# Seven block products in place of eight for 18 of 22 weight pairs of the second feed-forward input

## Chip, core and metric

The kernel runs on one NeuronCore of a Trainium2 chip (TensorE = PE, VectorE = DVE, ScalarE = ACT, GpSimd = POOL, SyncE = SP). The metric is the device time in microseconds (us) of one execution, lower is better; the median of several runs counts.

## The reference

One layer of a hybrid backbone on 128 context tokens and 512 noisy tokens, 640 columns in all, each of width 1024. The layer is a first SwiGLU feed-forward block, a mixer (short convolution and gated DeltaNet), and a second SwiGLU block, each with a modulated RMS norm ahead and a gated residual behind. The change lies in the second block:

```python
def _swiglu(h, w_in, w_out):
    a, b = jnp.split(h @ w_in, 2, axis=-1)
    return (jax.nn.silu(a) * b) @ w_out
...
    h = _rmsnorm(x, norm_ffn2) * (1 + sc3) + sh3
    x = x + 0.5 * gt3 * _swiglu(h, w_ffn2_in, w_ffn2_out)
```

`w_ffn2_in` is 1024 by 5632 (a and b of 2816 columns each), `w_ffn2_out` is 2816 by 1024. All is float32.

## The kernel before

Activations lie transposed: features on the 128 partitions, the 640 tokens as columns, so a feature vector of 1024 is KD = 8 tiles and the inner width 2816 is KF = 22 tiles. Float32 accuracy comes from splitting each operand in a high part (`_hi`, rounded to PE's fast float32r form) and a low part (`_lo`, the rest), and adding three products: hi*hi, hi*lo and lo*hi.

A **unit** is one column tile of weights (128 columns, all 8 k tiles): `load_w` (SP, L335) brings 512 KB into a slot of `w_raw`, `split_hi` (ACT, L942) and `split_lo` (DVE, L1266) make `w_hi` and `w_lo`, and `unit` (PE, L521) issues 8 k tiles * 3 products * 2 halves of the tokens = 48 matmuls:

```python
for n, (w, m) in enumerate(((wh, hi), (wh, lo), (wl, hi))):
    for b in range(2):
        last = pe.matmul(to[a_slot][b], w, m[:, k0 + k, part[b]],
```

The two halves (320 columns and 322) go to two PSUM banks in turn. The columns past the 640th hold the norm's shift, so the norm's scale 1/rms can be applied after the product. There are two weight slots and two accumulators.

A **pair** is unit a and unit b of the same 128 inner features. For a pair, DVE multiplies both results with `rinv` out of PSUM (`scaled`, L1336, two instructions for each unit), ACT takes silu with the shift as bias (`gate_in`, L1018), and DVE forms (b + shift) * silu (`shifted`, L1354), then g_hi (L1376) and g_lo (L1378). The second block's input stage is 22 such pairs, in a hardware loop from pair 2 on. Each engine's order is that of the code; semaphores (`mm_done`, `hi_ready`, `lo_ready`, `acc_free`) hold the engines together.

The stage opens with `sum_squares(2)` (L536) after its first unit and `spread(2)` (L543) after its second, by which 1/rms gets onto all partitions; ACT copies it out (L995, L996). The **output stage** (`swiglu_out`) follows: for each of 8 output tiles j three weight units of 8, 7 and 7 k tiles, 132 matmuls, then five transposes of the tile before (`turn_y`, L923). For j = 0 each k tile waits until its g_hi and g_lo are there (`g_rdy`).

Of the kernel before, what the change touches and what calls it, by code (L numbers as in the profile page):

```python
# [45 lines left out]
KO = ((0, 8), (8, 15), (15, 22))  # L46
HEADS = 4
# [23 lines left out]
U_F2O = U_F2I + 2 * KF  # L71
# [7 lines left out]
A_F2O = A_F2I + 2 * KF  # L79
# [31 lines left out]
def hybrid_layer(nc, x_prompt, x_sample, state_f, state_b, c, c_ctx, w_ada, b_ada, norm1, w1i, w1o, norm_mix,  # L111
# [3 lines left out]
    with ctx:  # L115
# [107 lines left out]
        def view(t, dims):  # L223
# [15 lines left out]

        ps = [ctx.enter_context(nc.psum_tensor(f"ps{i}", [P, 512], F32)) for i in range(8)]  # L240
# [18 lines left out]
        misc_set, vec_tr, vec_rdy, c_rdy = sem("misc_set"), sem("vec_tr"), sem("vec_rdy"), sem("c_rdy")  # L259
# [67 lines left out]
        def _(sp):  # L327
# [87 lines left out]
            for n in range(28):  # L415
                col = strip_col(n)
                load_w(U_MI + n, n % 2, w_mi_v[:, :, col:col + P], KD)
                if n == 1:
# [9 lines left out]
                                 ).then_inc(in_adt, 16)  # L428
                    sp.dma_start(gsm["adt"][:, 8:16], dt_bias.rearrange("a b h -> a (b h)").to_broadcast([P, 8])
                                 ).then_inc(in_adt, 16)  # L430
# [65 lines left out]
            with sp.Fori(0, KF) as i:  # L496
                for b in range(2):
                    load_w(U_F2I + 2 * i + b, b, w_in_v[1][:, :, bass.ds(P * i + b * FF, P)], KD)
            load_out(U_F2O, w_out_v[1])
# [4 lines left out]
            sp.wait_ge(out_done, 16 * NC)  # L504
            sp.wait_ge(st_done, 32)
# [3 lines left out]
        def _(pe):  # L509
            def unit(u, slot, kt, hi, lo, a_slot, start=True, stop=True, k0=0, h_wait=None, wide=True, ks=None):  # L510
# [3 lines left out]
                for k in ks or range(kt):  # L514
# [4 lines left out]
                    for n, (w, m) in enumerate(((wh, hi), (wh, lo), (wl, hi))):  # L519
                        for b in range(2):  # L520
                            last = pe.matmul(to[a_slot][b], w, m[:, k0 + k, part[b]],  # L521
                                             start=start and k == 0 and n == 0,
                                             stop=stop and k == kt - 1 and n == 2)
                last.then_inc(mm_done, 1)
# [51 lines left out]
            pe.wait_ge(c_rdy, 1)  # L576
# [60 lines left out]
            def swiglu_out(u0, a0, g0, after=lambda j: None):  # L637
                for j in range(KD):
                    s = j % 2
                    acc_wait(a0 // 2 + j // 2, s)  # L640
# [5 lines left out]
            swiglu_out(U_F1O, A_F1O, 0)  # L646
# [37 lines left out]
            for n in range(2, 28):  # L684
# [21 lines left out]
                if n == 12:  # L706
# [5 lines left out]
                    last.then_inc(ab_tr, 1)  # L712
                if n == 14:

                    pe.wait_ge(dve_g, 1)
                    pe.wait_ge(in_tri, 48)
# [192 lines left out]
            unit(U_F2I + 1, 1, KD, h_hi, h_lo, 1)  # L909
            spread(2)  # L910
# [3 lines left out]
            with pe.Fori(2, KF) as i:  # L914
                swiglu_in(i, U_F2I, A_F2I)

# [10 lines left out]
            swiglu_out(U_F2O, A_F2O, KF, after=lambda j: turn_y(j - 1) if j > 0 else None)  # L927
# [4 lines left out]
            last.then_inc(y_sum, 1)  # L932
# [3 lines left out]
        def _(act):  # L936
# [11 lines left out]
            for row, v in ((R_N1, norm1[0]), (R_NM, norm_mix[0]), (R_N2, norm2[0]), (R_NF, norm_f)):  # L948
# [14 lines left out]
                                 ).then_inc(c_rdy, 1)  # L963
# [79 lines left out]
            def swiglu_out(u0, n0, more, x0, after):  # L1043
                for j in range(KD):
                    split_out(u0, 3 * j + 1)
# [29 lines left out]
            for n in range(28):  # L1075
# [4 lines left out]
                if n == 13:  # L1080

                    act.wait_ge(ab_rdy, 3)
                    nc.scalar.activation(gsm["t1"][:, :, :, :], gsm["t1"][:, :, :, :], ACT.Exp).then_inc(act_g, 1)
                    nc.scalar.activation(gsm["beta"][:, :, :, :], gsm["t3"][:, :, :, :], ACT.Exp).then_inc(act_g, 1)
                    act.wait_ge(in_adt, 32)
# [4 lines left out]
                if n == 15:  # L1090
                    act.wait_ge(dve_g, 2)
                    nc.scalar.activation(gsm["gl"][:, :, :, :], gsm["gt"][:, :, :, :], ACT.Exp)
                    nc.scalar.activation(gsm["kgs"][:, :, :, :], gsm["t2"][:, :, :, :], ACT.Exp).then_inc(gates, 1)  # L1093
# [70 lines left out]
            for n in range(-1, NC):  # L1164
# [7 lines left out]
                if n == 0:  # L1172
# [4 lines left out]
                    for d, out in enumerate((s_out_f, s_out_b)):  # L1177
                        act.wait_ge(s_rdy[d], 1)
                        act.dma_start(out[0, 0].rearrange("h k v -> k h v"), Sb[d][:, :, :]).then_inc(st_done, 16)
# [27 lines left out]
            act.wait_ge(st_done, 32)  # L1207
# [53 lines left out]
        def _(dve):  # L1261
# [192 lines left out]
            def gates_first():  # L1454

                dve.wait_ge(ab_tr, 1)
                dve.wait_ge(in_adt, 32)
                ab4 = G["ab"][:, :].rearrange("p (c a h) -> p a c h", c=NC, a=4)
                link(nc.vector.tensor_copy(G["ab"][:, :], ps[6][:, 0:NC * NAB]))
                for d in range(2):  # L1460
# [5 lines left out]
                                        ).then_inc(ab_rdy, 1)  # L1466
# [436 lines left out]
```

## Time and profile before

| | |
|---|---|
| three runs, us | 1514.38, 1517.43, 1517.10 (median 1517.1) |
| the profiled execution, us | 1514.96 |
| its span in the trace, us | 1513.1 |
| PE busy | 1445.8 us, 96% of the span |
| DVE busy | 690.1 us, 46% |
| ACT busy | 401.7 us, 27% |
| SP's hardware DMA queue | 153.06 MB, 32.7% of 16 engines |
| mean granted PE clock | 0.979 |

An engine's busy time is the time in which it had an instruction under way; matmuls overlap, so PE's rate is read from the distance between starts or from the length of a run of matmuls. The clock is given as a share of 2.4 GHz. A number in square brackets behind a row of the timeline is the time that the engine stood idle before it, with what ended it.

### The profile page before, as it was taken

How to read it: one execution, taken by the hardware profiler on the slowest of the kernel's cores; microseconds unless marked ns; L12 is line 12 of the kernel's file. 1: busy time of each engine (PE TensorE's matmuls, PEld its weight loads, DVE VectorE, ACT ScalarE, POOL GpSimd, SP SyncE). 2: the span in 40 equal slices, each digit the busy share in tenths (PEclk: the TensorE clock that was granted, in tenths of full speed). 3: DMA queues.
4: the chain of work that ended last, by engine and by line, in shares of the span. 5: the costliest groups of instructions: out<-in, count | busy, mean ns of one | idle time of the engine just before them, and what ended most of it. 6: DMA issues, size and time to landing. Idle time of an engine off the chain costs nothing.

```text
span 1513.1 us, 24131 instructions
## 1 busy us (share of the span) xinstructions
PE 1445.8 (96%) x9932; PEld 1398.4 (92%) x9932; DVE 690.1 (46%) x1203; ACT 401.7 (27%) x596; POOL 112.9 (7%) x92
## 2 busy tenths in 40 slices
PE   5899999999999999999987999899999999999996
PEld 2787899999999999999986999899999999999996
DVE  2433344444323326566476665554444354442222
ACT  3321112122122226553222212232221221222222
POOL 0000000000000000002342664000000000000000
PEclk9899999999999999999998999999999999999998
DMA  9687522222222222222544333021222222222222
GB/s 342 247 297 274 166 67 80 68 73 74 72 77 77 74 72 70 70 57 84 158 135 124 104 91 88 15 84 57 83 69 69 83 69 69 83 63 77 77 67 80
DMA packets 221459, 154.73 MB, mean 102 GB/s; under 512 B 22437, under 2 KB 208206, under 8 KB 217294
## 3 DMA queue, kind: packets, MB, share of 16 engines
q1 hardware_dynamic: 219936, 153.06, 32.7%
q8 instruction: 52, 0.85, 0.2%
q10 hardware_dynamic: 1454, 0.68, 0.2%
q14 instruction: 17, 0.14, 0.0%
HBM read 140.47 MB, written 13.24 MB: 102 GB/s over the span
## 4 chain that ended last, share of the span: by engine, by line
PE 90%; DVE 4%; DMA 1%; ACT 1%; POOL 1%; issue 1%; SPq 1%; ACTq 0%; DVEq 0%; POOLq 0%
PE ps L521 72%; PE ps L883 3%; PE ps L563 2%; PE ps L755 2%; PE ps L767 1%; PE ps L766 1%; PE ps L594 1%; DMA w_raw<-in_w_ffn_in 1%; DVE sub_tmp L1534 1%; PE ps L869 1%; PE ps L802 1%; DVE sub_x L1537 1%; POOL Tm L1834 1%; DVE ss L1610 1%; PE ps L804 1%
## 5 line engine op out<-in xcount | busy, mean ns | idle before, releaser
L521 PE MATMUL ps<-h_hi,w_hi 128*128 128x320 f32 (+1 forms) x1824 | 427.1, 315 | 3.1 <-DVE w_lo L1266 3.1
L521 PE MATMUL ps<-h_lo,w_hi 128*128 128x320 f32 (+1 forms) x1824 | 421.7, 312 | 0.0
L521 PE MATMUL ps<-h_hi,w_lo 128*128 128x320 f32 (+1 forms) x1824 | 420.4, 312 | 0.0
L942 ACT ACTIVATE w_hi<-w_raw 128x1024 fp32r<-128x1024 f32 (+1 forms) x172 | 178.7, 1040 | 808.4 <-PE ps L521 742.9
L521 PEld LDWEIGHTS ps<-h_hi,w_hi 128*128 128x128 f32 x1824 | 310.0, 190 | 17.0 <-issue 12.9
L521 PEld LDWEIGHTS ps<-h_hi,w_lo 128*128 128x128 f32 x1824 | 309.9, 190 | 0.0
L521 PEld LDWEIGHTS ps<-h_lo,w_hi 128*128 128x128 f32 x1824 | 309.2, 190 | 0.0
L1266 DVE TENSOR_TENSOR w_lo<-w_raw,w_hi 128x1024 fp32r<-128x1024 f32 (+1 forms) x172 | 207.9, 1209 | 185.3 <-ACT w_hi L942 181.5
L1336 DVE TENSOR_TENSOR pn<-ps,rinv 128x320 f32<-128x320 f32 (+1 forms) x144 | 64.1, 487 | 274.3 <-PE ps L521 263.5
L521 PE MATMUL ps<-g_hi,w_hi 128*128 128x320 f32 x704 | 160.7, 310 | 0.0
L521 PE MATMUL ps<-g_hi,w_lo 128*128 128x320 f32 x704 | 160.5, 309 | 0.0
L521 PE MATMUL ps<-g_lo,w_hi 128*128 128x320 f32 x704 | 160.5, 309 | 0.0
L521 PEld LDWEIGHTS ps<-g_hi,w_lo 128*128 128x128 f32 x704 | 117.8, 188 | 0.0
L521 PEld LDWEIGHTS ps<-g_hi,w_hi 128*128 128x128 f32 x704 | 117.6, 188 | 0.0
L521 PEld LDWEIGHTS ps<-g_lo,w_hi 128*128 128x128 f32 x704 | 117.5, 188 | 0.0
L1336 DVE TENSOR_TENSOR sa<-ps,rinv 128x320 f32<-128x320 f32 x88 | 39.2, 487 | 133.5 <-PE ps L521 115.1
L1406 DVE SCALAR_TENSOR_TENSOR x<-ps,gate,x 128x128 f32<-128x128 f32 (+2 forms) x72 | 27.2, 434 | 89.8 <-PE ps L521 66.9
L1816 POOL TENSOR_TENSOR DT<-tri,s_g 128x512 f32<-128x512 f32 x10 | 11.3, 1138 | 754.6 <-ACT s_kgs L1093 686.7
L1354 DVE SCALAR_TENSOR_TENSOR pn<-pn,sa 128x128 f32<-128x128 f32 x88 | 44.7, 549 | 4.3 <-ACT sa L1018 1.1
L1171 ACT ACTIVATE Xm<-ps 128x512 f32<-128x512 f32 x30 | 17.9, 597 | 99.3 <-PE ps L755 99.3
L1018 ACT ACTIVATE sa<-sa 128x128 f32<-128x128 f32 x88 | 44.1, 548 | 0.0
L767 PE MATMUL ps<-Rm,Xm 128*128 128x128 f32 x240 | 41.5, 279 | 0.0
(233 smaller groups left out, 1289.2 us busy)
## 6 DMA issues: line engine op xcount, KB each, us to landing
w_raw<-in_w_ffn_in SPq DMA_DIRECT2D x88, 512.0 KB, 3.7
ada_w<-in_w_ada SPq DMA_DIRECT2D x32, 1024.0 KB, 6.5
w_raw<-in_w_ffn_out SPq DMA_DIRECT2D x32, 448.0 KB, 3.5
w_raw<-in_w_mix_in SPq DMA_DIRECT2D x28, 512.0 KB, 3.7
w_raw<-in_w_ffn_out SPq DMA_DIRECT2D x16, 512.0 KB, 3.8
ada_w<-in_w_ada SPq DMA_DIRECT2D x8, 512.0 KB, 4.0
w_raw<-in_w_mix_out SPq DMA_DIRECT2D x8, 512.0 KB, 5.1
d_lt<-LTp SPq DMA_DIRECT2D x10, 256.0 KB, 2.2
```

The source lines that it names most:

```text
L521: last = pe.matmul(to[a_slot][b], w, m[:, k0 + k, part[b]], start=start and k == 0 and n == 0, stop=stop and k == kt - 1 and n == 2)
L563: last = pe.matmul(adap[32 * g:32 * g + 32, 0:width], ccol[:, k, :], ada_w[:, s, g * width:(g + 1) * width], start=k == 0, stop=k == KD - 1)
L755: last = pe.matmul(hs(bank[d][3], h), nt[:, h, :], Tm[d][:, h, :], start=True, stop=True)
L767: last = pe.matmul(hs(bank[d][2], h), Xm[d][:, h, :], R[:, h, :], start=True, stop=True)
L883: last = pe.matmul(acc[s][b], w, m[:, k % 4, PART[b]], start=k == 0 and n == 0, stop=k == KD - 1 and n == 2)
L942: nc.scalar.activation(w_hi[:, slot, 0:kt * P], w_raw[:, slot, 0:kt * P], ACT.Copy).then_inc(hi_ready, 1)
L1018: last = nc.scalar.activation(sa[:, t0:t1], sa[:, t0:t1], ACT.Silu, bias=sa[:, T + g:T + g + 1])
L1171: nc.scalar.activation(flat(Xm[d]), bank[d][3][:, :], ACT.Copy).then_inc(xm_rdy[d], 1)
L1266: nc.vector.tensor_tensor(w_lo[:, slot, 0:kt * P], w_raw[:, slot, 0:kt * P], w_hi[:, slot, 0:kt * P].bitcast(F32), ALU.subtract).then_inc( ...
L1336: last = nc.vector.tensor_tensor(dst[:, PARTW[b]], accw[a_slot][b], rinv[:, PARTW[b]], ALU.mult)
L1354: last = nc.vector.scalar_tensor_tensor(out=dst[:, t0:t1], in0=pn[:, t0:t1], scalar=pn[:, T + g:T + g + 1], in1=other[:, t0:t1], op0=ALU.a ...
L1406: last = nc.vector.scalar_tensor_tensor(out=x[:, j, t0:t0 + b1 - b0], in0=acc[a_slot][bnk][:, b0:b1], scalar=gate[:, m, j, i:i + 1], in1=x ...
```

## The change

The first NP0 = 4 pairs stay as they are. The other NSP = 18 pairs are each computed as a 2 by 2 block product: the weights in halves of k (0 to 3, 4 to 7) and in a and b, the activations in the same halves of k and in the two token halves (320 each). Seven products of 4 k tiles and 320 columns take the place of eight (Strassen's scheme in Winograd's form): 7 * 4 * 3 = 84 matmuls for a pair in place of 96. They need four sums of weight blocks for each pair (`S1` to `S4f`, DVE), four sums of activation blocks made once (`T1` to `T4`, DVE), and sums of products: five on DVE out of PSUM (u2, u3, c22, c21, c12), and three in PSUM, where products 4, 5 and 6 accumulate on the banks of products 0, 2 and 3. ACT copies product 0 out first (p1), and takes silu of c11 and c12.

For that the normed, scaled and shifted h must exist in float32 (`hf`): during the first four pairs DVE multiplies x by 1/rms (8 of 640 columns) and ACT applies gain and shift (16 instructions). Each of the seven activation operands is split in hi and lo once (1280 columns), each of the seven weight operands for every pair (512 columns each).

The weights of even pairs load into `w_raw`, those of odd pairs into `w_more` (a part of the old `h` buffers), as two DMAs of 512 KB each. Eight PSUM banks serve two pairs in turn, four each. The product g stays float32 (`g32`) through the stage, one DVE multiplication of 640 columns for a pair; hi and lo of all 22 tiles are made at the end (`halve_hi` on ACT, `halve_lo` on DVE, 22 each), partly over the memory of the block operands. Some semaphores of other stages are merged, with the waits at the same places. `spread(2)` moves into the middle of the second unit.

```diff
-            with pe.Fori(2, KF) as i:
+            for i in range(2, NP0):
                 swiglu_in(i, U_F2I, A_F2I)
+            def product(s, p, to, w, v, again=False):
+                pe.wait_ge(op_rdy, 7 * s + (p + 1))
+                for k in range(4):
+                    wh, wl = (t[:, k * P:k * P + P] for t in w[0:2])
+                    for n, (a, m) in enumerate(((wh, v[0]), (wh, v[1]), (wl, v[0]))):
+                        last = pe.matmul(to, a, m[:, k, :], start=not again and k == 0 and n == 0, stop=k == 3 and n == 2,
+                                         skip_group_check=again)
+                last.then_inc(pr_done, 1)
...
+                product(s, 0, X, A11, b11_g if first else B11)
...
+                product(s, 1, Y, S2, T2)
...
+                product(s, 2, Z, S3, T3)
...
+                product(s, 3, W, S1, T1)
+                pe.wait_ge(*p1_rdy(s))
...
+                product(s, 4, X, A12, B21, again=True)
+                pe.wait_ge(*u3_rdy(s))
+                product(s, 5, Z, A22, T4, again=True)
+                pe.wait_ge(*c22_rdy(s))
...
+                product(s, 6, W, S4, B22, again=True)
```

SP and DVE (the first load of a block pair waits for the last `split_lo` of the old form):

```diff
+            sp.wait_ge(lo_ready, U_F2O)
+            load_pair(0, 0, first(0))
...
+            sums_of(0, 0, None)
+            part_lo(3, T4, T4[2][:, :, :])
+            last_sum(0, 0)
+            unit_scaled(6, 0)
+            part_lo(4, b11_g, block(0, 0))
+            operand_lo(0, 0, A11, w_raw[:, 0, 0:HW4])
...
+            for k in range(0, 6):
+                halve_lo(k)
+            dve.wait_ge(pr_done, 7 * NSP)
+            nc.vector.tensor_tensor(c12, u2, xyzw[1][3], ALU.add).then_inc(dve_ev, 1)
+            split_out(U_F2O, 0)
...
+            split_out(U_F2O, 1)
+            for k in range(12, KF):
+                halve_lo(k)
```

What DVE does for a pair inside its loop. Before, one pass of the loop (`sa`, `pn` results of a and b, `w_lo` the two weight units, `g` the product):

```order
L1266 TENSOR_TENSOR w_lo<-w_raw,w_hi 128x1024 [waits hi_ready]
L1361 REGISTER_ALU
L1336 TENSOR_TENSOR sa<-ps,rinv 128x320 [waits mm_done]
L1336 TENSOR_TENSOR sa<-ps,rinv 128x322
L1265 REGISTER_ALU
L1266 TENSOR_TENSOR w_lo<-w_raw,w_hi 128x1024 [waits hi_ready]
L1336 TENSOR_TENSOR pn<-ps,rinv 128x320 [waits mm_done]
L1336 TENSOR_TENSOR pn<-ps,rinv 128x322
```

In the change, the first part of one pair (`sa` here is c12 of the pair before; `rinv` is u2, `S_` and `A_` are weight operands, `g_171` is g32):

```order
L2111 TENSOR_TENSOR sa<-rinv,ps 128x320 [waits pr_done]
L2091 REGISTER_ALU
L2092 TENSOR_TENSOR S_lo<-S_sum,S_hi 128x512 [waits oh_rdy]
L2091 REGISTER_ALU
L2092 TENSOR_TENSOR A_lo<-w_raw,A_hi 128x512 [waits oh_rdy]
L2096 REGISTER_ALU
L2097 REGISTER_ALU [waits act_ev]
L2098 REGISTER_ALU [waits act_ev]
L2103 ISA [waits dve_ev]
L2103 TENSOR_TENSOR g_171<-sa,pn 128x640
L2117 ISA [waits pr_done]
L2121 REGISTER_ALU [waits act_ev]
```

Longer instructions have become shorter ones with more register steps and waits between them; a whole pair has 17 DVE instructions that compute.

DVE at the seam to the output stage. Before, the last rows of the loop and the first behind it:

```order
L1378 REGISTER_ALU [waits gh_rdy]
L1378 TENSOR_TENSOR g_lo<-pn,g_hi 128x640
L1778 REGISTER_ALU
L1778 COMPARE_AND_BRANCH
L1266 TENSOR_TENSOR w_lo<-w_raw,w_hi 128x896 [waits hi_ready] x2
```

In the change, from the last pair's c21 on:

```order
L2143 TENSOR_TENSOR pn<-rinv,ps 128x320 [waits pr_done]
L2166 TENSOR_TENSOR g_lo<-g_171,g_hi 128x640 [waits gh_rdy] x6
L2172 TENSOR_TENSOR sa<-rinv,ps 128x320 [waits pr_done]
L1503 TENSOR_TENSOR w_lo<-w_raw,w_hi 128x1024 [waits hi_ready]
L2166 TENSOR_TENSOR g_lo<-g_171,g_hi 128x640 [waits gh_rdy] x3
L2103 TENSOR_TENSOR g_171<-sa,pn 128x640 [waits dve_ev,act_ev]
L2166 TENSOR_TENSOR g_lo<-g_171,g_hi 128x640 [waits gh_rdy] x3
L1503 TENSOR_TENSOR w_lo<-w_raw,w_hi 128x896 [waits hi_ready]
L2166 TENSOR_TENSOR g_lo<-g_171,g_hi 128x640 [waits gh_rdy] x10
L1503 TENSOR_TENSOR w_lo<-w_raw,w_hi 128x896 [waits hi_ready]
```

The low part of the output stage's first weight unit (the first `w_lo` row) now stands behind six g_lo and the sum c12, and 16 more g_lo follow it.

## Rows read from the trace of the kernel before

**Rows 1.** The page, chain that ended last: shares of the span by engine and line.
```profile
PE 90%; DVE 4%; DMA 1%; ACT 1%; POOL 1%; issue 1%; SPq 1%; ACTq 0%; DVEq 0%; POOLq 0%
PE ps L521 72%; PE ps L883 3%; PE ps L563 2%; PE ps L755 2%; PE ps L767 1%; PE ps L766 1%; PE ps L594 1%; DMA w_raw<-in_w_ffn_in 1%; DVE sub_tmp L1534 1%; PE ps L869 1%; PE ps L802 1%; DVE sub_x L1537 1%; POOL Tm L1834 1%; DVE ss L1610 1%; PE ps L804 1%
```

**Rows 2.** Windows: stretch, us, then busy of each engine, granted clock, DMA share, GB/s.
```profile
1075.00:1210.00 135.00, 135.00 (x910) 135.00 (x909) 60.35 (x93) 29.16 (x39) 0.00 (x0) 1.00 0.26 76
```

**Rows 3.** Timeline of DVE, one pair of the loop: start, length, instruction, idle before.
```profile
1303.42 0.89 DVE L1336 TENSOR_TENSOR sa<-ps,rinv 128x320 f32<-128x320 f32 x2 [2.39 <-PE ps L521]
1304.51 1.22 DVE L1266 TENSOR_TENSOR w_lo<-w_raw,w_hi 128x1024 fp32r<-128x1024 f32 x1 [0.20 <-ACT w_hi L942]
1310.56 0.89 DVE L1336 TENSOR_TENSOR pn<-ps,rinv 128x320 f32<-128x320 f32 x2 [4.82 <-PE ps L521]
1311.57 1.02 DVE L1354 SCALAR_TENSOR_TENSOR pn<-pn,sa 128x128 f32<-128x128 f32 x2
1312.73 0.49 DVE L1376 CAST g_hi<-pn 128x640 f32 x1
1313.34 0.82 DVE L1378 TENSOR_TENSOR g_lo<-pn,g_hi 128x640 f32 x1
1314.09 1.22 DVE L1266 TENSOR_TENSOR w_lo<-w_raw,w_hi 128x1024 fp32r<-128x1024 f32 x1
1317.70 0.49 DVE L1336 TENSOR_TENSOR sa<-ps,rinv 128x320 f32<-128x320 f32 x1 [2.39 <-PE ps L521]
```

**Rows 4.** The chain in order of time, output stage: start, us, what.
```profile
1377.79 0.55 PE ps L923 x5
1378.34 19.36 PE ps L521 x132
1397.70 0.55 PE ps L923 x5
```

**Rows 5.** Groups by form, 640 us to the end: count, busy us, mean ns, idle before.
```profile
L1266 DVE TENSOR_TENSOR w_lo<-w_raw,w_hi 128x1024 fp32r<-128x1024 f32 x76 | 94.6, 1246 | 45.9 <-ACT w_hi L942 44.8
L1336 DVE TENSOR_TENSOR pn<-ps,rinv 128x320 f32<-128x320 f32 x40 | 19.6, 491 | 141.0 <-PE ps L521 139.3 <-issue 1.6
L1378 DVE TENSOR_TENSOR g_lo<-pn,g_hi 128x640 f32 x20 | 16.5, 825 | 2.5
L1703 DVE TENSOR_TENSOR Rm<-Rm,ps 128x512 f32<-128x512 f32 x30 | 20.3, 682 | 6.4 <-PE ps L767 6.3
L1171 ACT ACTIVATE Xm<-ps 128x512 f32<-128x512 f32 x30 | 17.9, 597 | 99.3 <-PE ps L755 99.3
```

**Rows 6.** The page, DMA issues: count, KB each, us to landing.
```profile
w_raw<-in_w_ffn_in SPq DMA_DIRECT2D x88, 512.0 KB, 3.7
ada_w<-in_w_ada SPq DMA_DIRECT2D x32, 1024.0 KB, 6.5
```

**Rows 7.** Timeline at the opening of the second block's input stage.
```profile
1037.76 1.23 PEld L543 LDWEIGHTS ps<-ident,rms 128*128 128x128 f32 x10
1039.22 0.60 ACT L995 ACTIVATE rinv<-ps 128x512 f32<-128x512 f32 x1 [7.14 <-PE ps L543]
1039.71 0.27 ACT L996 ACTIVATE rinv<-ps 128x128 f32<-128x128 f32 x1
```

**Rows 8.** Timeline of PE: two waits elsewhere in the kernel.
```profile
569.57 0.78 PE L521 MATMUL ps<-h_hi,w_hi 128*128 128x320 f32 x2 [3.06 <-DVE w_lo L1266]
826.38 2.05 PE L755 MATMUL ps<-Tm,NTa 128*128 128x128 f32 x8 [5.58 <-POOL NTa L1843]
```

**Rows 9.** Windows behind those two waits, columns as in rows 2.
```profile
570.00:575.00 5.00, 5.00 (x26) 5.00 (x25) 3.02 (x7) 4.07 (x6) 0.00 (x0) 0.69 0.37 105
826.00:832.00 6.00, 5.43 (x24) 5.17 (x25) 0.00 (x0) 1.19 (x2) 6.00 (x6) 0.50 0.27 55
832.00:836.00 4.00, 4.00 (x34) 3.92 (x33) 2.04 (x4) 0.00 (x0) 4.00 (x5) 0.93 0.06 15
```

**Rows 10.** Timeline of PE, products in plain float32 (two instructions each, same columns).
```profile
889.92 2.01 PE L767 MATMUL ps<-Rm,Xm 128*128 128x128 f32 x16
```

More of the change, by code:

```diff
@@ L908, in _ @@
             acc_wait(A_F2I // 2, 1)
-            unit(U_F2I + 1, 1, KD, h_hi, h_lo, 1)
-            spread(2)
+            unit(U_F2I + 1, 1, KD, h_hi, h_lo, 1, between=lambda k: spread(2) if k == 3 else None)
             unit(U_F2I + 2, 0, KD, h_hi, h_lo, 2)
@@ new lines, in hi_last, with seven @@
+            def hi_last(s, q, free):
+                act.wait_ge(*free[0])
+                operand_hi(s, 5, A22, (w_raw, w_more)[q][:, 1, HW4:])
+                act.wait_ge(*free[1])
+                act.wait_ge(sum_rdy, 4 * s + 4)
+                operand_hi(s, 6, S4, S4f[:, :])
+            def seven(s, q, prep=True):
+                X, Y, Z, W = xyzw[q]
+                first = isinstance(s, int) and s == 0
+                if not first:
+                    act.wait_ge(*c12_rdy(s - 1))
+                    nc.scalar.activation(c12, c12, ACT.Silu).then_inc(act_ev, 1)
+                act.wait_ge(pr_done, 7 * s + 1)
+                if not first:
+                    act.wait_ge(*u2_rdy(s - 1))
+                nc.scalar.activation(p1, X, ACT.Copy).then_inc(act_ev, 1)
+                hi_last(s, q, ((mm_done, U_F2O),) * 2 if first else ((pr_done, 7 * s - 1), (pr_done, 7 * s)))
+                if first:
+                    part_hi(5, B21, hf[:, 4:KD, 0:TH])
+                    part_hi(6, B22, hf[:, 4:KD, TH:T])
+                    for i in range(2):
+                        act.wait_ge(vlo, 5)
+                        nc.scalar.activation(B11[i][:, :, :], b11_g[i][:, :, :].bitcast(F32), ACT.Copy).then_inc(vhi, 1)
+                if prep:
+                    hi_a11(s + 1, 1 - q, (pr_done, 7 * s + 1))
+                act.wait_ge(pr_done, 7 * s + 5)
+                act.wait_ge(*g_made(s + (NP0 - 1)))
+                nc.scalar.activation(c11, X, ACT.Silu).then_inc(act_ev, 1)
+                if prep:
+                    hi_four(s + 1, 1 - q, (pr_done, 7 * s + 5))
@@ new lines, in _, with halve_hi @@
+            hi_a11(0, 0, (mm_done, U_F2O - 1))
+            gate_in(3, A_F2I, KF)
+            hi_four(0, 0, (mm_done, U_F2O - 1))
+            seven(0, 0)
+            with act.Fori(0, NSP // 2 - 1) as r:
+                for q in (1, 0):
+                    seven(2 * r + (2 - q), q)
+            seven(NSP - 1, 1, prep=False)
+            def halve_hi(k):
+                last = 7 * (NSP - 1)
+                act.wait_ge(pr_done, last + (2 if k < 4 else 3 if k < 8 else 4 if k < 12 else 6))
+                if k >= 20:
+                    act.wait_ge(op_rdy, 7 * NSP)
+                act.wait_ge(*g_made(k))
+                nc.scalar.activation(g2_hi[:, k, :], g32[:, k, :], ACT.Copy).then_inc(gh_rdy, 1)
```

400 lines of the change are left out of this document (336 added, 64 removed).

## The prediction

> **What bounds the kernel now.** I read the chain that ended last first [rows 1]: 90% of it is PE, 72% the matmuls of L521, so what counts is how many matmuls there are, how far apart they start, and where PE waits. The window in the middle of the stage that changes [rows 2] shows PE busy for all of its 135 us at the full clock of 2.4 GHz, DVE for 60 us and ACT for 29. The timeline of DVE [rows 3] gives the period of a pair, from one result `sa` to the next: 1317.70 - 1303.42 = 14.28 us for 96 matmuls, 148.75 ns each (320 and 322 columns in turn). In the output stage, where all have 320 columns, 132 take 19.36 us [rows 4]: 146.67 ns each. The profiled execution took 1514.96 us, its span 1513.1; the median of the three runs, 1517.1, is 2.1 above it.
>
> **What the change takes from PE.** A block pair has 84 matmuls of 320 columns: 84 * 0.14667 = 12.32 us for 14.28, that is 1.96 us less; for 18 pairs **-35.3 us**, if PE stays without waits. That prices the same 128-row weight load and the same float32r columns as in rows 4. What differs is that the 12 matmuls of a product follow each other in one bank, where now two banks alternate. The trace has no float32r row of that. In the nearest rows [rows 10] a plain float32 product is two instructions into the same columns of a bank, 16 in 2.01 us, 115 ns each and no gap. So I take 0, between a gain of 0 and the loss of the second rival. TensorE's own rate is also the place to weigh a rule: the Trainium skill, page "TensorE: Matmul & The Clock Gate", section "Back-to-back issue gap", gives columns / 2.4 GHz + 2.5 ns, 135.8 ns for 320 columns. Rows 4 show 146.67. By the page the pair would save 13.08 - 11.41 = 1.67 us and the stage 30.1; I stay with the rows.
>
> **Does DVE keep up inside the loop?** A block pair has 17 computing DVE instructions. Five sums out of PSUM at 0.49 us, one product of 640 columns at 0.825 [rows 5]; eleven of 512 columns out of SBUF (four sums, seven low parts), priced at 0.70, between the 0.682 of a 512-column operation with a PSUM operand and the line through 640 and 1024 columns (0.825 and 1.246) [rows 5]. Sum 2.45 + 0.825 + 7.7 = 10.97 us, against 12.32 of PE. Back to back it is less: independent neighbours overlap by about 0.07 (w_lo starts at 1314.09, g_lo would end at 1314.16) [rows 3], so 9.8. ACT has seven copies of 512 at 0.60 and three of 320 at about 0.5: 5.7 us. I laid the three engines' orders side by side with these durations, 0.1 us from one of them to the next and 0.2 from PE or to PE. Counted from a pair's product 0: c12 at 0.2, S1 and A12 low parts by 1.9, the g product by 2.7, u2 at 3.7 (product 1 ends at 3.5), u3 at 5.5, c22 at 7.2, S1, S3, S2, the next pair's A11 and S4f by 10.8, c21, S2 and S3 low parts by 12.5. The next product 0 needs A11's low part, ready at 10.2, at 12.3; product 1 needs S2's at 14.1, ready at 11.9. Everything is about 2 us early, each pair alike, so in the loop **0**. Weights: a pair's load starts 4.9 us into the pair but one before it, and is wanted at 20.0, 15 us later; two DMAs of 512 KB in series would take 2 * 3.7 = 7.4 [rows 6]. Hidden, with half the time to spare.
>
> **The opening.** `spread(2)` moves, its cost (1.2 us of PE) stays. But DVE now does `scaled` for unit 0 and two of the x * 1/rms before it makes w_lo of unit 2. Spread ends 3.57 us of matmuls before unit 1 does; ACT copies 1/rms out in about 0.8 [rows 7]; then 0.89 + 2 * 0.755 + 1.16 on DVE (each less its overlap) and 0.2 to PE, 4.9 us against 3.57: **+1.3**.
>
> **The seam into the block pairs.** The first block load is issued only when the last w_lo of the old form is made, about 9.4 us before unit 7, the last old one, ends. For its two DMAs of 512 KB I take the 6.5 us of the row of 1024 KB, between 3.7 (all in parallel) and 7.4 (in series) [rows 6]. Behind it DVE has S1, S3, S2 (2.0), T4's low part (1280 columns, 1.42), S4f (0.63), `scaled` (0.82), B11's low part (1.42), A11's (0.63), in all 6.9, and 0.3 for the hand-overs: 6.5 + 6.9 + 0.3 - 9.4 = **+4.3** in front of product 0 (1.5 to 5.2). Product 4 then waits for B21's low part: **+0.55**.
>
> **The seam to the output stage.** Let E be the end of the last product. DVE's c21 starts at E - 1.56 (product 5 is done), ends at about E - 1.15; six g_lo at 0.755 take it to E + 3.4, c12 to E + 3.8, w_lo (1.16) to E + 5.0. PE starts at **+5.2**; before, it started at once. Then PE takes 0.88 us for a k tile, DVE 0.755 for a g_lo, but it has the last g product and w_lo of the second unit in between, and w_lo of the third comes behind g_lo 21, at E + 19.9, where PE wants it at E + 18.4 (k tile 15): **+1.7**. The 22 g_lo and casts that leave the loop are in these terms; in the loop they were hidden. The cover for all of this is the matmuls of j = 0; it is too short by 1.7.
>
> **The clock.** Waits of that size have a second price. After 3.06 us of waiting [rows 8] the granted clock was 0.69 in the next 5 us, with 26 matmuls [rows 9], where 5 / 0.14875 = 33.6 fit: 1.1 us lost. After 5.58 us [rows 8] it was 0.50 for 6 us and 0.93 for the next four [rows 9], 1.2 GHz for some 6.3 us; 320 columns at 1.2 GHz are 267 ns, for 147, so 6.3 * (1 - 147/267) = 2.8 lost. I take 1.1 for the wait of 4.3 and 2.8 for that of 5.2. A slow PE lets DVE catch up, so the small waits behind them (0.55, 1.7) vanish: net 3.9 - 2.25 = **+1.7**.
>
> **The sum:** -35.3 + 1.3 + 4.3 + 0.55 + 5.2 + 1.7 + 1.7 = -20.5, so 1514.96 - 20.5 = 1494.4. Because the profiled execution lies 2.1 below the median, I add half of that: **1495.5 us**. Merged semaphores and earlier stages cost nothing; their waits stand where they stood. That the change does less than it says is excluded: 216 fewer matmuls are issued.
>
> **Rivals.** A measurement of this kernel can tell about 0.2%, 3 us, from no change.
>
> *DVE becomes the bound in the loop, and the kernel slower.* For: in the loop DVE's dependent instructions start 0.12 to 0.15 us after their forerunner's end (1311.57, 1312.73, 1313.34) [rows 3], with one register step and one wait between; the new loop has up to four. If every one of the 17 pays such a gap of 0.2 and overlaps nothing, a pair is 10.97 + 3.4 = 14.4 us, the gain 35.3 - 18 * 2.05 = -1.6, and with the seams' 14.8 the kernel takes 1532. The kernel gets slower from a period of 14.28 - 14.8/18 = 13.5, a gap of 0.15. Against: the one independent follower in the loop, w_lo with its wait already fulfilled, shows no gap but an overlap, and in the new order each dependent pair has another instruction between. The Trainium skill, page "VectorE: DVE Perf Modes", section "The TRN2 errata", states a fixed extra cost for each instruction, so that many small ones pay more; by it this rival is likelier than the one row makes it. 9%.
>
> *One bank for 12 matmuls costs PE time.* 1512 matmuls; 25 ns each would be +38, 1533 us, and 14 ns already take the whole gain. Against it stand rows 10 without a gap. 3%.
>
> *Partly bound.* A gap of 0.1 without overlap makes DVE's period 12.7, +6; with somewhat slower cross-engine steps, seams of 18 to 20 us in all and a longer slow clock this ends between 1502 and 1513, say 1506. 17%.
>
> *Shorter seams.* The first load lands in 3.7 us, no clock falls at the first wait, DVE overlaps more: 1485 to 1489. 7%.
>
> **How the numbers follow.** Forecast 62% (1489 to 1502 by the load's ends and the clock's), shorter seams 7%, partly bound 17%, back to within 0.2% of before 2%, slower 12% (9 and 3). So faster 0.86, same 0.02, slower 0.12. The range leaves out the slower cases and some of the partly bound at the top, and the very best at the bottom: 1486 to 1511.
>
> **What would show it.** Pairs 12.3 us apart in the new loop and PE without idle time there; DVE busy for about 9.8 us of each. Three waits of PE: about 1.3 before unit 2, 4 before the first block product (released by a low part of DVE after a weight load), 5 before the output stage (released by w_lo). Granted clock below 1 behind the last two. The output stage from j = 1 on as in rows 4. Wrong would be: a period over 12.6 us; waits on `op_rdy` in every pair; 84 matmuls that take over 12.4 us without idle time (the bank); or seams of more than 20 us.

## The result, and the profile after

| | before | changed |
|---|---|---|
| median, us | 1517.26 (4 runs, 1514.38 to 1518.69) | 1492.64 (4 runs, 1489.5 to 1493.57) |
| ratio to before | | 0.9835, 95% interval 0.9819 to 0.9851 |
| the profiled execution, us | 1514.96 | 1493.57 |
| its span, us | 1513.1 | 1491.8 |
| PE busy, us | 1445.8 | 1416.8 |
| DVE, ACT busy, us | 690.1, 401.7 | 779.5, 472.0 |
| mean granted PE clock | 0.979 | 0.975 |

The change makes the kernel 1.65% faster. The forecast was 1495.5, in a range of 1486 to 1511.

The chain that ended last, changed kernel, from the stage's first unit to the output stage (start, us, what; it answers to [rows 4]):

```profile
1024.00 7.14 PE ps L583 x48
1032.15 3.68 PE ps L583 x24
1075.26 5.02 DMA w_raw<-in_w_ffn_in
1087.15 8.73 PE ps L986 x48
1096.14 212.99 PE ps L986 x1452
1309.65 4.41 DVE g_lo L2166 x6
1315.84 40.40 PE ps L583 x264
1356.79 19.36 PE ps L583 x132
```

L986 is the block product, L583 every other feed-forward matmul. The row of 1452 carries the gain: 212.99 / 1452 = 146.69 ns a matmul, without a break over 17 pairs. The chain leaves PE for long only twice, for the first block load and for the six g_lo with the w_lo behind them. The shares in the profile page's chain say the same: PE fell from 90% [rows 1] to 88%, DVE rose from 4% to 5%.

PE's waits in the stage, from its timeline (the bracket is the idle time before, with its releaser; the kernel before had no waits at these places):

```profile
1041.33 0.56 PE L583 MATMUL ps<-h_hi,w_hi 128*128 128x320 f32 x2 [0.80 <-DVE w_lo L1503]
1087.15 0.60 PE L986 MATMUL ps<-b_hi,A_hi 128*128 128x320 f32 x1 [2.71 <-DVE A_lo L2092]
1096.14 0.39 PE L986 MATMUL ps<-B_hi,A_hi 128*128 128x320 f32 x1 [0.27 <-issue]
1315.84 0.87 PE L583 MATMUL ps<-g_hi,w_hi 128*128 128x320 f32 x2 [4.96 <-DVE w_lo L1503]
```

Windows of the changed kernel, columns as in [rows 2]: the two places behind the long waits, and the middle of the loop.

```profile
1087.00:1090.00 3.00, 2.85 (x11) 2.88 (x12) 2.96 (x7) 1.13 (x3) 0.00 (x0) 0.50 0.86 239
1130.00:1290.00 160.00, 160.00 (x1094) 160.00 (x1093) 126.16 (x221) 66.37 (x131) 0.00 (x0) 1.00 0.30 85
1315.80:1319.80 4.00, 3.96 (x17) 3.99 (x18) 4.00 (x6) 4.00 (x7) 0.00 (x0) 0.59 0.39 115
```

In the loop PE is busy for all of the 160 us at the full clock, as in [rows 2], with DVE at 79% where it had 45%. Behind both waits the granted clock is 0.50 to 0.59 in these windows, that is 1.2 GHz for most of them, and matmuls run 267 ns apart (in product 0 from 1087.55 to 1087.82 and on): product 0 takes 1090.44 - 1087.15 = 3.29 us, the first 12 of the output stage as much (1315.84 to 1319.13). Each time that is 1.53 us more than 12 * 0.14667 = 1.76. This is what one execution shows; the experiments below show that the price of the clock isn't the same in each.

DVE in the loop, one pair from c12 (`sa`) on, which answers to [rows 3]:

```profile
1163.24 0.49 DVE L2111 TENSOR_TENSOR sa<-rinv,ps 128x320 f32<-128x320 f32 x1
1163.64 0.68 DVE L2092 TENSOR_TENSOR S_lo<-S_sum,S_hi 128x512 fp32r<-128x512 f32 x1
1164.24 0.68 DVE L2092 TENSOR_TENSOR A_lo<-w_raw,A_hi 128x512 fp32r<-128x512 f32 x1
1164.85 0.82 DVE L2103 TENSOR_TENSOR g<-sa,pn 128x640 f32 x1
1167.06 0.49 DVE L2122 TENSOR_TENSOR rinv<-ssq,ps 128x320 f32<-128x320 f32 x1 [1.39 <-PE ps L986]
1167.46 0.68 DVE L2092 TENSOR_TENSOR A_lo<-w_raw,A_hi 128x512 fp32r<-128x512 f32 x1
1168.70 0.49 DVE L2128 TENSOR_TENSOR rinv<-rinv,ps 128x320 f32<-128x320 f32 x1 [0.55 <-PE ps L986]
1169.10 0.68 DVE L2092 TENSOR_TENSOR S_lo<-S4f,S_hi 128x512 fp32r<-128x512 f32 x1
1170.45 0.49 DVE L2135 TENSOR_TENSOR pn<-rinv,ps 128x320 f32<-128x320 f32 x1 [0.66 <-PE ps L986]
```

DVE stands idle 1.39 + 0.55 + 0.66 = 2.6 us a pair, always for a product, never for ACT or a load. An instruction of 512 columns lasts 0.68, but the next starts 0.60 behind it (1163.64, 1164.24). The register steps and the fulfilled waits between them (each pair of rows here has them) take no time that the timeline shows. Such gaps were what the slower rival rested on. The Trainium skill, page "VectorE: DVE Perf Modes", section "The DRAIN you can't avoid", says that a semaphore after each DVE instruction costs nothing extra; the trace agrees, with 0.60 a step across such waits.

**Where the time went**, against the kernel before. Its stage starts at 1022.68 (chain) and its unit 2 at 1038.94 (timeline of PE):

```profile
1022.68 7.14 PE ps L521 x48
1038.94 0.54 PE L521 MATMUL ps<-h_hi,w_hi 128*128 128x320 f32 x2
```

(The profiled execution of the changed one enters the stage 1.3 us later, 1024.00 against 1022.68; the versions below, which differ in nothing ahead of it, enter it anywhere from 1021.51 to 1025.30.)

| step | us | worked out |
|---|---|---|
| 1512 matmuls for 1728 | -35.3 | 18 * (14.28 - 12.32) |
| unit 2's wait | +1.07 | starts 17.33 after the stage's first unit, before 16.26 |
| wait before product 0 | +2.98 | unit 7 would have ended at 1041.33 + 6 * 7.14 = 1084.17, product 0 starts at 1087.15 |
| slow clock there | +1.53 | 3.29 for 1.76 |
| B21's low part | +0.27 | the row at 1096.14, see e_dve_a |
| wait before the output stage | +5.0 | the row at 1315.84 |
| slow clock there | +1.53 | 3.29 for 1.76 |
| sum | -22.9 | |

From the stage's first unit to the first `turn_y` (the five transposes, L923 before, L1036 now) the chains give 1377.79 - 1022.68 = 355.11 and 1356.25 - 1024.00 = 332.25: -22.86. So the sum leaves nothing of this execution unexplained. I call this stretch the **stage length**. It is read from one profiled execution of each kernel. It doesn't hold what whole executions differ by ahead of the stage and behind it, so it is the sharper measure below: the same kernel gives 332.25 and 332.00 (again), or 324.44 and 324.47 (v_all, v_all_b). It does hold the clock, which can move it by a microsecond or more.

### The profile page after: what moved, and what is told of

The parts are those of the page before. It is cut to its first block, busy times and chain, and to the rows that moved or that the text cites. A ratio compares the mean times of both kernels' runs of the same rounds, so it can differ in the third digit from the quotient of the medians.

```text
span 1491.8 us, 24430 instructions
## 1 busy us (share of the span) xinstructions
PE 1416.8 (95%) x9716; PEld 1368.1 (92%) x9716; DVE 779.5 (52%) x1362; ACT 472.0 (32%) x751; POOL 112.9 (8%) x92
## 4 chain that ended last, share of the span: by engine, by line
PE 88%; DVE 5%; DMA 2%; POOL 1%; ACT 1%; issue 1%; SPq 1%; ACTq 0%; DVEq 0%; POOLq 0%
PE ps L583 55%; PE ps L986 15%; PE ps L947 3%; PE ps L626 2%; PE ps L819 2%; PE ps L831 1%; PE ps L830 1%; DMA w_raw<-in_w_ffn_in 1%; PE ps L657 1%; DVE sub_tmp L1772 1%; PE ps L933 1%; PE ps L866 1%; POOL Tm L2236 1%; DVE sub_x L1775 1%; DVE w_lo L1503 1%
## 5 line engine op out<-in xcount | busy, mean ns | idle before, releaser
L583 PE MATMUL ps<-h_hi,w_hi 128*128 128x320 f32 x1248 | 295.1, 318 | 3.9 <-DVE w_lo L1503 3.9
L583 PE MATMUL ps<-h_lo,w_hi 128*128 128x320 f32 x1248 | 288.6, 313 | 0.0
L583 PE MATMUL ps<-h_hi,w_lo 128*128 128x320 f32 x1248 | 288.3, 312 | 0.0
L583 PEld LDWEIGHTS ps<-h_hi,w_hi 128*128 128x128 f32 x1248 | 212.5, 190 | 18.0 <-issue 12.9
L583 PEld LDWEIGHTS ps<-h_hi,w_lo 128*128 128x128 f32 x1248 | 212.5, 190 | 0.0
L583 PEld LDWEIGHTS ps<-h_lo,w_hi 128*128 128x128 f32 x1248 | 211.9, 190 | 0.0
L583 PE MATMUL ps<-g_hi,w_hi 128*128 128x320 f32 x704 | 161.6, 311 | 5.0 <-DVE w_lo L1503 5.0
L583 PE MATMUL ps<-g_hi,w_lo 128*128 128x320 f32 x704 | 160.9, 310 | 0.0
L583 PE MATMUL ps<-g_lo,w_hi 128*128 128x320 f32 x704 | 160.8, 310 | 0.0
L1573 DVE TENSOR_TENSOR pn<-ps,rinv 128x320 f32<-128x320 f32 x108 | 48.1, 487 | 173.7 <-PE ps L583 162.8
L583 PEld LDWEIGHTS ps<-g_hi,w_hi 128*128 128x128 f32 x704 | 118.1, 189 | 5.2 <-issue 5.2
L583 PEld LDWEIGHTS ps<-g_lo,w_hi 128*128 128x128 f32 x704 | 118.3, 189 | 0.0
L583 PEld LDWEIGHTS ps<-g_hi,w_lo 128*128 128x128 f32 x704 | 118.1, 189 | 0.0
L986 PE MATMUL ps<-T_hi,S_hi 128*128 128x320 f32 x216 | 66.7, 309 | 0.0
L986 PE MATMUL ps<-T_hi,S_lo 128*128 128x320 f32 x216 | 66.7, 309 | 0.0
L986 PE MATMUL ps<-T_lo,S_hi 128*128 128x320 f32 x216 | 66.7, 309 | 0.0
```

What stands on the lines that cost most here:

```text
L583: last = pe.matmul(to[a_slot][b], w, m[:, k0 + k, part[b]], start=start and k == 0 and n == 0, stop=stop and k == kt - 1 and n == 2)
L986: last = pe.matmul(to, a, m[:, k, :], start=not again and k == 0 and n == 0, stop=k == 3 and n == 2, skip_group_check=again)
L1573: last = nc.vector.tensor_tensor(dst[:, PARTW[b]], accw[a_slot][b], rinv[:, PARTW[b]], ALU.mult)
```

## Experiments

All were run on chips with the kernel before beside them. Ratios are to that kernel, with the 95% interval. There were three groups: again, e_inseam, e_outseam and v_all (before: 1515.94); e_dve_a, e_dve_b, e_eight and e_open (1517.05); v_all2 and v_all_b (1516.96).

| run | median, us | ratio | stage length, us |
|---|---|---|---|
| again | 1493.7 | 0.9843 (0.983 to 0.9857) | 332.00 |
| e_dve_a | 1493.39 | 0.9846 (0.9822 to 0.9871) | 333.02 |
| e_dve_b | 1510.34 | 0.9958 (0.994 to 0.9976) | 348.71 |
| e_eight | 1523.15 | 1.0046 (1.003 to 1.0061) | 360.78 |
| e_open | 1493.07 | 0.9844 (0.9821 to 0.9867) | 331.97 |
| e_inseam | 1489.23 | 0.9825 (0.9812 to 0.9838) | 327.74 |
| e_outseam | 1489.29 | 0.9822 (0.9803 to 0.9841) | 328.94 |
| v_all | 1485.72 | 0.9799 (0.9786 to 0.9813) | 324.44 |
| v_all_b | 1487.1 | 0.9799 (0.9776 to 0.9823) | 324.47 |
| v_all2 | 1482.06 | 0.9773 (0.9752 to 0.9793) | 320.98 |

**again**, the changed kernel unedited, as the base of the others.

> The changed kernel once more, as the yardstick of this chip. Both theories: ratio to before about 0.984 to 0.986 (24.6 us less by the medians so far, 21.4 by the profiled executions); in the trace again three waits of PE in the second input stage, about 0.8, 2.7 and 5.0 us, and a loop period of 12.3 us.

It repeats: 1493.7, with the same waits (0.80, 2.5, 5.0).

### Is the loop bound by PE, and by how much?

**e_dve_a and e_dve_b**: a reduction on DVE in every pair, 1500 or 3600 columns, whose result nobody reads.

```diff
                 if not first:
                     gate_pair(s - 1)
+                nc.vector.tensor_reduce(ssq[:, TH:TH + 1], x[:, :, :].rearrange("p k t -> p (k t)")[:, 0:3600],
+                                        mybir.AxisListType.X, ALU.add)
                 dve.wait_ge(pr_done, 7 * s + 2)
```

> One more DVE instruction in each of the 18 block pairs, behind the g product: a sum over 1500 columns of x into a spare column, about 1.6 us, whose result nobody uses. Forecast's theory (DVE has 2.6 us to spare in a period of 12.3 and the operands are 2 us early): no more than 2 us slower in all, period 12.3. Rival (DVE near its bound): period 13 or more, 12 us slower or more.

> The same with 3600 columns, about 3.8 us. Forecast's theory: DVE's 9.8 us become 13.6, so DVE is the bound, period 13.6 us, PE waits in every pair, about 23 us slower than the changed kernel, which is the time of the kernel before (1513 to 1520). A theory in which waits between the engines add to the sums gives 14 us and more for a pair, over 30 us slower.

The small one costs nothing that can be measured, though DVE's busy time in the middle of the loop rises from 126.16 to 146.04 of 160 us. The window of e_dve_a:

```profile
1130.00:1290.00 160.00, 160.00 (x1094) 160.00 (x1093) 146.04 (x235) 66.32 (x130) 0.00 (x0) 1.00 0.30 85
```

The stage length is 1.0 longer than in again, but not by waits of PE for the loaded DVE: the clock makes the difference. The chain of e_dve_a has these two rows, where the changed kernel has 8.73 and 40.40:

```profile
1086.06 7.28 PE ps L986 x48
1314.50 41.55 PE ps L583 x264
```

The waits before them are nearly those of the change (2.58 for 2.71, and 4.96), but the granted clock isn't: behind the first it stayed at 1.00, and behind the second it was 0.50 until 5.7 us after the restart, where in the change it was back at 1.00 after 3.2. The first saves 1.45 us, the second costs 1.15. (e_eight below has 7.28 at the first place too, behind a wait of 2.68.)

What the load on DVE does cost is in the first pair, ahead of product 4. There PE waits 1.48 us where the change had 0.27, both times put down to "issue". DVE's timeline names the releaser: B21's low part ends at 1093.23 + 1.48 = 1094.71 in e_dve_a, and product 4 starts at 1094.82; from the timelines of DVE and of PE in e_dve_a,

```profile
1093.23 1.48 DVE L2040 TENSOR_TENSOR B_lo<-hf,B_hi 128x1280 fp32r<-128x1280 f32 x1
```

```profile
1094.82 0.39 PE L986 MATMUL ps<-B_hi,A_hi 128*128 128x320 f32 x1 [1.48 <-issue]
```

In the changed kernel that low part runs from 1094.56 to 1096.04, and product 4 starts 0.10 behind its end, at 1096.14. In e_dve_b it ends at 1098.46 and the product starts at 1098.57. So the 0.27 is the prediction's wait for B21, and "issue" here is a wait whose releaser the profile didn't find.

Set against the changed kernel's own profile (333.02 for 332.25, 0.8 longer), e_dve_a has 1.21 more for this wait, 0.13 less for the wait before product 0, 1.45 less and 1.15 more for the clock. From product 4 on the loop costs nothing more: 1452 matmuls take 212.98 us in e_dve_a and 212.99 in the change.

With the large one DVE is busy for all of the window, PE is not, and PE waits once in every pair. First the same window of e_dve_b, then its rows of PE's waits in the stage (engine line <- releaser: us in total, times, longest us):

```profile
1130.00:1290.00 160.00, 153.06 (x1025) 149.94 (x1024) 160.00 (x221) 61.23 (x123) 0.00 (x0) 1.00 0.28 80
```

```profile
PE ps L986 <- DVE rinv L2130: 9.6, 17, 0.7
PE ps L583 <- ACT sa L1480: 5.0, 1, 5.0
```

The wait before the output stage stays at 5.0, under another releaser. The period is 13.16 us in place of 12.32. From the timeline of DVE in e_dve_b:

```profile
1147.31 3.89 DVE L2116 TENSOR_REDUCE ssq<-x 128x1 f32<-128x3600 f32 x1
1151.13 0.47 DVE L2124 TENSOR_TENSOR rinv<-ssq,ps 128x320 f32<-128x320 f32 x1
...
1160.47 3.89 DVE L2116 TENSOR_REDUCE ssq<-x 128x1 f32<-128x3600 f32 x1
```

The reduction takes 1151.13 - 1147.31 = 3.82 of the period, so the pair's own 17 instructions, packed with nothing idle, take 13.16 - 3.82 = 9.34 us. The prediction had 9.8, and the same excess is why this run came out below the 1513 to 1520 that it was expected to take. In the loop of the change DVE could thus do 12.32 - 9.34 = 3.0 us more for each pair (worked out; e_dve_a takes about 1.6 of it at no cost, and the 3.82 of e_dve_b are too much).

**e_eight**: 12 more matmuls a pair, ahead of product 6. One of the four results of a pair is therefore another one.

```diff
+                for k in range(4):
+                    wh, wl = (t[:, k * P:k * P + P] for t in A22[0:2])
+                    for a, m in ((wh, T4[0]), (wh, T4[1]), (wl, T4[0])):
+                        pe.matmul(W, a, m[:, k, :], start=False, stop=False, skip_group_check=True)
                 product(s, 6, W, S4, B22, again=True)
```

> Twelve more matmuls in each block pair, as an eighth product would have: A22 and T4 once more, into the bank of product 6, so that one of the four results is another one. Forecast's theory (PE's matmuls are all that the loop costs, one bank or not): 18 * 1.76 = 31.7 us slower than the changed kernel, period 14.08, no waits in the loop. If the loop had hidden slack of its own on another engine, less: 25 or below.

The chain of e_eight in the loop is PE alone:

```profile
1280.55 12.31 PE ps L986 x84
1292.85 1.76 PE ps L1024 x12
```

An eighth product costs 1.76 us a pair in full; the kernel is then slower than before, by 0.46%. Of the 18 * 1.76 = 31.7 us the medians show 29.5 (1523.15 - 1493.7) and the stage length 28.8. The wait before the output stage is 3.2 here, not 5.0, since DVE gets 1.76 us more before the end, and in the profiled execution the clock didn't fall in the first seam (7.28 for 8.73). Together with e_dve_b this gives the point at which the kernel turns slower, too: ratios 0.9958 at a period of 13.16 and 1.0046 at 14.07 cross 1 at 13.16 + 0.91 * 42 / 88 = 13.6. The prediction put it at 13.5.

### The two seams

**e_inseam**: the low parts that need no weights come ahead of the weight sums.

```diff
-            sums_of(0, 0, None)
             part_lo(3, T4, T4[2][:, :, :])
-            last_sum(0, 0)
             unit_scaled(6, 0)
             part_lo(4, b11_g, block(0, 0))
+            sums_of(0, 0, None)
+            last_sum(0, 0)
```

> DVE makes the low parts of T4 and B11 and unit 6's result ahead of the first weight sums, while the first block load is in flight. Theory A (DVE's order behind the load makes the 2.7 us): the wait before the first block product goes to 0, and with it the slow clock of its 12 matmuls, together 4 to 4.5 us less than the changed kernel. Theory B (the load's landing sets the seam): sums start at the same time, but the wait stays over 1.5 us and less than 2 us is won.

The wait is gone, and no slow matmuls follow. The chain of e_inseam:

```profile
1039.01 43.11 PE ps L583 x288
1082.12 7.04 PE ps L986 x48
1089.15 0.27 issue
1089.42 212.99 PE ps L986 x1452
```

48 block matmuls take 7.04 us where the change took 8.73. The stage length falls by 332.0 - 327.74 = 4.3, against 2.98 + 1.53 = 4.5 in the table. The 0.27 of B21 stays. So the wait hung on DVE's order, as theory A had it. In the change DVE stands idle 4.10 us for the load and only then makes 1.48 + 1.48 us of low parts that don't need it:

```profile
1074.72 1.48 DVE L2040 TENSOR_TENSOR T_lo<-T_sum,T_hi 128x1280 fp32r<-128x1280 f32 x1
1080.30 0.69 DVE L2078 TENSOR_TENSOR S_sum<-w_raw 128x512 f32<-128x512 f32 x1 [4.10 <-DMA w_raw<-in_w_ffn_in]
...
1082.12 1.48 DVE L2040 TENSOR_TENSOR T_lo<-T_sum,T_hi 128x1280 fp32r<-128x1280 f32 x1
...
1084.92 1.48 DVE L2040 TENSOR_TENSOR b_lo<-hf,b_hi 128x1280 fp32r<-128x1280 f32 x1
```

**e_outseam**: in the last pair, ACT makes the high parts of six g tiles and of the first output unit ahead of c11; DVE makes three g_lo, that unit's low part and another g_lo ahead of c21. DVE's part of the edit:

```diff
+                else:
+                    for k in range(0, 3):
+                        halve_lo(k)
+                    split_out(U_F2O, 0)
+                    halve_lo(3)
                 dve.wait_ge(pr_done, 7 * s + 6)
...
-            for k in range(0, 6):
+            for k in range(4, 6):
                 halve_lo(k)
...
-            split_out(U_F2O, 0)
```

> The last pair makes the first six g_hi and the high part of the first output weight unit ahead of its c11 (ACT), and DVE makes four g_lo and that unit's low part ahead of its c21. Theory A (the wait of 5.0 us before the output stage is only DVE's order, and the slow clock behind it is its consequence): wait below 0.6, the first 12 matmuls of the output stage take 1.8 us and not 3.3, together 5.5 to 6.5 us less than the changed kernel. Theory B (DVE's total of 22 g_lo is too much for the cover, so the wait only moves to a later k tile of j = 0): a new wait of 3 us or more inside j = 0 and less than 3 us won.

The wait of 5.0 is gone and so is the slow clock, 6.5 us together. The medians show 4.4 of it (1493.7 - 1489.29), the stage length 3.1 (332.00 - 328.94), which is the number that the rows below account for. PE stops twice inside j = 0 instead; from its timeline in e_outseam:

```profile
1317.56 0.56 PE L583 MATMUL ps<-g_hi,w_hi 128*128 128x320 f32 x2 [1.01 <-DVE w_lo L1504]
1325.91 0.56 PE L583 MATMUL ps<-g_hi,w_hi 128*128 128x320 f32 x2 [1.93 <-DVE w_lo L1504]
```

These are the second and the third weight unit; with what PE needs to start again, the two take some 3.4 of the 6.5 back. The second of them is the prediction's wait at k tile 15 (1.7): in the change the late start and the slow clock had covered it, here nothing does. Both theories held in part. DVE's timeline of e_outseam shows why the units are late: each stands behind g_lo that PE needs after it.

```profile
1313.48 0.82 DVE L2104 TENSOR_TENSOR g<-sa,pn 128x640 f32<-128x640 f32 x1
1314.21 2.29 DVE L2108 TENSOR_TENSOR g_lo<-g,g_hi 128x640 fp32r<-128x640 f32 x3
1316.42 1.08 DVE L1504 TENSOR_TENSOR w_lo<-w_raw,w_hi 128x896 fp32r<-128x896 f32 x1
1317.42 7.44 DVE L2108 TENSOR_TENSOR g_lo<-g,g_hi 128x640 fp32r<-128x640 f32 x10
1324.78 2.22 DVE L1504 TENSOR_TENSOR w_lo<-w_raw,w_hi 128x896 fp32r<-128x896 f32 x2
```

**e_open**: w_lo of unit 2 ahead of the second x * 1/rms.

```diff
             normed(0)
-            normed(1)
             split_lo(U_F2I + 2, 0, KD)
+            normed(1)
             unit_scaled(1, 1)
```

> Only the opening: DVE makes w_lo of unit 2 ahead of the second x * 1/rms. Theory A (one DVE instruction too many ahead of it): PE starts unit 2 about 0.75 us earlier. Theory B (ACT's copy of 1/rms or its high part of unit 2 is last): no change.

Unit 2 starts 16.59 us into the stage where the change had 17.33, the 0.74 of theory A. But another wait comes two units later, since ACT makes w_hi of unit 4 behind the `hf` parts that now have their input later:

```profile
1054.99 0.53 PE L583 MATMUL ps<-h_hi,w_hi 128*128 128x320 f32 x2 [0.30 <-DVE w_lo L1503]
```

Product 0 starts 62.91 us into the stage, against 62.98 to 63.15 in the six others that have the wait there and the old opening (the change, again, e_outseam, e_dve_a, e_dve_b, e_eight): nothing that can be told from chance. Where the seam behind it is mended as well, v_all has product 0 at 60.23 and e_inseam at 60.44, so the opening's edit is worth some 0.2 us.

### All of it together

**v_all** has the three edits (e_inseam, e_outseam, e_open), and A11's low part ahead of S4f.

> Both seams as in the two experiments before, A11's low part ahead of S4f, and w_lo of unit 2 ahead of the second x * 1/rms at the opening. Theory A: no wait of PE over 0.4 us from the second unit of the stage to the end of j = 0, full clock throughout, 10 to 11.5 us less than the changed kernel (about 1481 by its median). Theory B: 4 us less at most.

It is 8.0 us faster than again, and 7.6 by the stage length, between what the two theories gave: the parts add up (4.3 + 3.1 and a little), the two waits inside j = 0 stay.

**v_all2** takes these away: on DVE the second unit's low part comes behind g tile 8, the third's behind g tile 14, and ACT's high parts to match. DVE's part of the edit, against v_all:

```diff
             for k in range(6, 9):
                 halve_lo(k)
+            split_out(U_F2O, 1)
             gate_pair(NSP - 1)
-            for k in range(9, 12):
+            for k in range(9, 15):
                 halve_lo(k)
-            split_out(U_F2O, 1)
-            for k in range(12, KF):
+            split_out(U_F2O, 2)
+            for k in range(15, KF):
                 halve_lo(k)
```

> v_all with two more pieces moved in the output stage's first block: the low part of the second weight unit comes on DVE right behind the ninth split of g (k tile 8) instead of behind the twelfth and the last pair's gate product, and that of the third unit behind the fifteenth instead of behind all 22, with their high parts on ACT to match. Theory A (the two waits that v_all has left there, 1.01 us at k tile 8 and 1.93 us at k tile 15 with their restarts, come from DVE's order alone, since DVE makes one k tile of g in 0.73 us where PE eats it in 0.88): both go, PE runs from the last product of the last pair into j = 0 and through its 132 matmuls in 19.4 us without a gap over 0.2 us; 1482 to 1483.5 us where v_all shows 1485.7. Theory B (DVE's total work in this stretch is what bounds it, so a wait moves rather than goes): a wait of 1 to 3 us comes behind k tile 9 or 15 on g_lo, and the time stays within 1 us of v_all.

> The same kernel as v_all, on the same chip as v_all2, for the comparison of the two: 8 us (6.5 to 9.5) under the changed kernel of before on its ratio, 0.979 to 0.982 of the kernel before.

Theory A held. The chain of v_all2 has PE alone from the loop through j = 0 and j = 1, 264 matmuls in 264 * 0.14667 = 38.72 us:

```profile
1083.84 7.04 PE ps L986 x48
1090.87 0.27 issue
1091.14 214.73 PE ps L986 x1464
1305.87 38.72 PE ps L583 x264
```

1482.06 us against 1487.1 of v_all_b beside it; the stage length says 324.47 - 320.98 = 3.5, the two waits of 1.01 and 1.93 with their restarts. v_all2 is the fastest of all, 0.9773 of the kernel before. Its stage is 34.1 us shorter than before, of the 35.3 that the matmuls alone give. So the work on DVE was never too much for the seams, it stood in the wrong order.

## Why the prediction was right

The sum was -20.5 and came out as -22.9 in the stage. The mechanism was right: PE bound in the loop, two seams on DVE's order and a slow clock behind them. Step by step:

- **PE's matmuls, -35.3**: right. 146.69 ns a matmul in the row of 1452, the 146.67 of [rows 4]. 12 matmuls in one bank cost nothing, so that rival falls. The isolated gap of the Trainium skill (page "TensorE: Matmul & The Clock Gate", section "Back-to-back issue gap") gives 135.8 ns at the full clock, 10.9 less than both kernels show; at the lower clock its 320 / 1.2 = 266.7 ns is the 267 of product 0.
- **The loop, 0**: right, and shown. DVE's own work is 9.34 us a pair (forecast 9.8), the period 12.32, and e_dve_a's load leaves it there. The slower rival's price was right as well (break-even 13.6 for 13.5), but not its cause. No gap follows a register step or a fulfilled wait. In [rows 3] the 0.12 to 0.15 stand between instructions of which the second reads what the first has just written. In the new loop another instruction stands between such two, as the prediction had it. Small instructions do cost a fixed part more, but little: 512 columns step in 0.60 us and 640 in 0.735 (six g_lo in 4.41), which leaves about 0.06 us for each instruction (an estimate from these two). The prediction's 0.70 for 512 columns was also a little high by its own rows: it is said to lie between 0.682 and the line through 640 and 1024 columns, but that line gives 0.685. Measured: 0.68.
- **The opening, +1.3**: 1.07. e_open shows that it mostly can't be had back by moving unit 2's low part.
- **The seam into the block pairs, +4.3**: 2.98. The mis-sized term is the load. I took 6.5 us from the row of 1024 KB; the two DMAs of 512 KB landed in 5.02, with 0.43 for SP's issue ahead of it (1074.83 to 1075.26) that the sum had no term for. DVE's part behind it took 6.71 for 6.9. With these, 0.43 + 5.02 + 6.71 + 0.16 for the hand-overs - 9.34 gives the 2.98.
- **B21's low part, +0.55, and k tile 15, +1.7**: the first is 0.27, with the slow clock ahead of it or without (e_inseam). The second was absorbed, as the clock step said; e_outseam shows it by itself, 1.93. The prediction missed a wait at the second unit (1.01), which the start 6.5 us late hides.
- **The seam to the output stage, +5.2**: 5.0.
- **The clock, net +1.7**: a term whose size came close by luck. That the clock can fall behind waits of this size is right, but the two falls were priced by the length of the wait, at 1.1 and 2.8, and length doesn't set the price. In the changed kernel's profile both cost 1.53, 3.06 for 3.9. In e_dve_a, with the same two waits, the first cost nothing and the second about 2.6 (41.55 - 38.72, less 0.24 for the restart as in 7.28 - 7.04). Clock and small waits together (3.95 forecast) are 3.06 + 0.27.

So -35.3 + 1.07 + 2.98 + 5.0 + 3.06 + 0.27 = -22.9, and of the 2.4 us between that and the forecast 1.3 are the first seam, 0.6 the clock and the small waits, 0.4 the two other waits. The medians lie 24.6 us apart, 1.7 more than the stage accounts for; that is within what single executions of one kernel differ by (1489.5 to 1493.57).

What stays open: it wasn't tried whether two pairs more of the old form, or all 22 in the new one, would do better. And what decides whether the clock falls behind a given wait, and for how long, isn't shown.

## What to carry to other kernels

Fewer matmuls pay in full only as long as the helping engine's work for one period fits into the shorter period, and its slack can be measured by putting useless work of a known length on it until PE begins to wait. A stage that changes its form costs at both seams, and there the order on the serial engine decides: list when each operand is wanted and make them in that order, with all that needs no late load ahead of it. A wait that is taken away uncovers the next one behind it, so the orders have to be mended through to the end of the work that hides them; three edits gave 8 us, and the fourth, of the waits that e_outseam had uncovered, 3.5 more. A slow clock behind a wait is a price with a range, not a number: one profile doesn't give it.

## What the hardware showed unexpectedly

- The same wait can cost a slow clock or nothing. Seven of the kernels have a wait of 2.5 to 2.7 us before product 0. In five the granted clock is 0.50 behind it and the next 48 matmuls take 8.65 to 8.75 us; in two (e_dve_a, 2.58, and e_eight, 2.68) it is 1.00 and they take 7.28. Behind the wait of 4.96 the 264 matmuls of j = 0 and j = 1 take 40.30 (e_inseam) to 41.55 us (e_dve_a), for 38.72 without a wait. In e_eight, behind 3.23, the clock fell only 1.2 us after PE had started again. Waits of 2.29 us and less were followed by the full rate in this stage: 72 matmuls in 10.81 us behind the 2.29 in e_dve_b, 174 in 25.78 behind the 1.93 in e_outseam.
- DVE instructions overlap by 0.08 us each across waits that are fulfilled: 0.49 steps in 0.40, 0.68 in 0.60. That makes 17 instructions with a summed length of 10.8 us fit into 9.34. Summing durations overstates a busy DVE by 15%.
